# Layer 1's projections in a new order, opened by token halves over two units of weights

## What is computed

```python
u  = _modulate(_rms_norm(h, norm_mix[l]), shm, scm)      # 256 tokens
uc = _modulate(_rms_norm(hc, norm_mix[l]), cshm, cscm)   # 256 context tokens
p = u @ w_in[l]                                          # queries, keys and values
q_w, q_g, q_n = _split_q(p[..., :1024])
k_w, v_w, k_g, v_g, k_n, v_n = _split_kv(p[..., 1024:])
kv_c = uc @ w_in[l][:, 1024:]                            # last layer: no queries of the context
q_g, k_g = _rms_norm(q_g, q_norm_glob[l]), _rms_norm(k_g, k_norm_glob[l])
ck_g = _rms_norm(ck_g, k_norm_glob[l])
q_w, k_w = _rope(q_w, cos, sin), _rope(k_w, cos, sin)
q_g, k_g = _rope(q_g, cos, sin), _rope(k_g, cos, sin)
...                                                      # window, global and neighbourhood attention
h = h + gm * (jnp.concatenate([y_w, y_g, y_n], axis=-1) @ w_out[l])
```

## Time and profile before

| what | value |
|---|---|
| median of 3 runs | 2045.58 us (2043.97 to 2045.92) |
| profiled execution, first to last instruction | 2042.0 us |
| around the span (median less span) | 3.6 us |
| PE busy | 1990.4 us, 97% of the span |
| DVE, ACT, POOL busy | 1410.1, 817.7, 221.7 us |
| mean granted TensorE clock | 0.993 of full speed |
| DMA | 314.41 MB, mean 154 GB/s |

### The profile page before, as it was taken

One profiled execution on the slowest core, in us unless ns is written; L12 is line 12 of the kernel. 1 busy time (PEld: TensorE's weight loads), 2 busy tenths in 40 slices (PEclk: granted clock), 3 DMA queues, 4 the chain that ended last, 5 costly groups with the idle time before them and its releaser, 6 DMA issues.

```text
span 2042.0 us, 28261 instructions
## 1 busy us (share of the span) xinstructions
PE 1990.4 (97%) x11270; PEld 1699.9 (83%) x11270; DVE 1410.1 (69%) x1985; ACT 817.7 (40%) x1182; POOL 221.7 (11%) x129
## 2 busy tenths in 40 slices
PE   8989999999999999999999999999999999999998
PEld 7977778888888887589888888988888888689998
DVE  6879997878867668845888867566664346865444
ACT  6353676222222336944222222322222234764443
POOL 0010001000001002520000001000000101333431
PEclk9999999999999999999999999999999999999999
DMA  6558994666545362024566555366654335125654
GB/s 200 160 171 267 300 347 116 188 178 186 162 137 166 116 166 70 2 63 114 156 185 177 152 160 151 84 175 195 187 164 131 91 114 162 42 83 145 186 164 146
DMA packets 415048, 314.41 MB, mean 154 GB/s; under 512 B 27559, under 2 KB 373686, under 8 KB 414918
## 3 DMA queue, kind: packets, MB, share of 16 engines
q1 hardware_dynamic: 375344, 236.97, 39.9%
q10 hardware_dynamic: 39574, 75.64, 12.0%
HBM read 311.52 MB, written 1.05 MB: 153 GB/s over the span
## 4 chain that ended last, share of the span: by engine, by line
PE 85%; DVE 8%; ACT 4%; issue 2%; DMA 1%; SPq 0%; DVEq 0%; ACTq 0%
PE ps L2311 25%; PE ps L2313 24%; PE ps L2312 24%; DVE w_lo L1340 3%; PE ps L2304 2%; PE ps L3156 2%; PE ps L3123 2%; ACT w_hi L779 1%; DVE ada_acc L1366 1%; DVE tmp_a L1425 1%; PE ps L2888 1%; DVE u_lo L1433 1%; PE ps L2890 1%; PE ps L2889 1%; PE ps L2919 1%
## 5 line engine op out<-in xcount | busy, mean ns | idle before, releaser
L2311 PE MATMUL ps<-u_hi,w_hi 128*128 128x512 f32 (+2 forms) x2112 | 736.5, 349 | 15.7 <-DVE u_lo L1433 7.7
L2312 PE MATMUL ps<-u_lo,w_hi 128*128 128x512 f32 (+2 forms) x2112 | 727.2, 344 | 0.0
L2313 PE MATMUL ps<-u_hi,w_lo 128*128 128x512 f32 (+2 forms) x2112 | 727.2, 344 | 0.0
L1340 DVE TENSOR_TENSOR w_lo<-raw,w_hi 128x2048 fp32r<-128x2048 f32 (+1 forms) x214 | 449.5, 2101 | 219.2 <-ACT w_hi L779 219.0
L779 ACT CAST w_hi<-raw 128x2048 fp32r<-128x2048 f32 (+1 forms) x213 | 371.0, 1743 | 413.3 <-PE ps L2313 379.0
L2311 PEld LDWEIGHTS ps<-u_hi,w_hi 128*128 128x128 f32 x2112 | 401.2, 190 | 70.3 <-DVE w_lo L1340 9.9
L2313 PEld LDWEIGHTS ps<-u_hi,w_lo 128*128 128x128 f32 x2112 | 401.2, 190 | 47.2
L2312 PEld LDWEIGHTS ps<-u_lo,w_hi 128*128 128x128 f32 x2112 | 401.4, 190 | 45.4
L1366 DVE SCALAR_TENSOR_TENSOR ada_acc<-ada_w,sc_c,ada_acc 128x512 f32<-128x512 f32 x448 | 318.0, 765 | 6.4 <-DVE ada_acc L1363 1.0
L899 ACT ACTIVATE tmp_a<-ps 128x512 f32<-128x512 f32 (+1 forms) x88 | 47.9, 544 | 559.6 <-PE ps L2313 417.7
L2311 PE MATMUL ps<-hf_hi,w_hi 128*128 128x512 f32 (+1 forms) x770 | 268.5, 349 | 0.1
(11 more groups left out here) (423 smaller groups left out, 2065.7 us busy)
## 6 DMA issues: line engine op xcount, KB each, us to landing
ada_w<-in_w_ada ACTq DMA_DIRECT2D x144, 512.0 KB, 3.8
raw<-in_w_ffn_gate SPq DMA_DIRECT2D x88, 512.0 KB, 4.0
raw<-in_w_ffn_up SPq DMA_DIRECT2D x88, 512.0 KB, 5.3
raw<-in_w_in SPq DMA_DIRECT2D x52, 512.0 KB, 5.0
raw<-in_w_ffn_down SPq DMA_DIRECT2D x64, 384.0 KB, 3.6
raw<-in_w_ffn_down SPq DMA_DIRECT2D x64, 320.0 KB, 4.2
raw<-in_w_expert_down SPq DMA_DIRECT2D x26, 512.0 KB, 6.3
raw<-in_w_expert_gate SPq DMA_DIRECT2D x25, 512.0 KB, 5.4
```

What stands on the lines that cost most here:

```text
L1340: tt(low, full, high.bitcast(F32), ALU.subtract).then_inc(lo_done.sem, 1)
L2311: mm(acc, w1, m_hi, start=(first and i == 0), stop=False)
L2312: mm(acc, w1, m_lo, start=False, stop=False)
L2313: ins = mm(acc, w2, m_hi, start=False, stop=(last and i == n - 1))
```

## The change

An explicit order of units replaces the natural one in layer 1: two key/value units (4 and 5), the four query units, the three other key/value units. Layer 0 keeps its order. In layer 1 the first two units are now 512 wide and are opened by `open_two`, as in layer 0; `second=False`, `CTX_ROWS` and both `context_rows` go. The groups `q` and `kv` keep their sizes, so `kv` now holds two query units and three key/value units, and the places of `att`, `sink` and the bias table in SP's queue stay behind the fourth and behind the seventh unit.

```diff
-        def taken_with(tile):
-            return 0 if tile < KA else (tile - KA) // 2 + 1
+        QKV_ORDER = [[0, 1, 2, 3, 4, 5, 6, 7, 8], [4, 5, 0, 1, 2, 3, 6, 7, 8]]
+        def taken_with(l, tile):
+            return max(QKV_ORDER[l].index(tile // 2) - 3, 0)
...
-        CTX_ROWS = ((0, 3), (3, 7), (7, 8), (8, 8))
...
-                linear(L["q"], a["w_in_2"][l], 0)
+                linear(L["q"], a["w_in_2"][l], 0, None, QKV_ORDER[l][0:4])
...
-                linear(L["kv"], a["w_in_2"][l], D, range(0, 3))
+                linear(L["kv"], a["w_in_2"][l], 0, range(0, 3), QKV_ORDER[l][4:])
...
-                linear(L["kv"], a["w_in_2"][l], D, range(3, 5))
+                linear(L["kv"], a["w_in_2"][l], 0, range(3, 5), QKV_ORDER[l][4:])
...
-                halves_norm(f"l{l}b", l, 3, end_of(L["f1b"]), next_two(L["f1b"]), second=not last)
-
-                def context_rows(i):
-                    k0, k1 = CTX_ROWS[i]
-                    high_rows("l1b", 72 + 24, 1, k0, k1)
-                linear(L["q"], ada=None if last else "q", behind=context_rows if last else None)
+                halves_norm(f"l{l}b", l, 3, end_of(L["f1b"]), next_two(L["f1b"]))
+                linear(L["q"], ada=None if last else "q")
...
+                def take(n, acc):
+                    i = QKV_ORDER[l][n]
+                    return to_queries(i, acc) if i < 4 else to_keys(i - 4, acc)
+
+                linear(L["q"], take, None if last else "q")
...
-                linear(L["kv"], to_keys, tail=None if last else 15, behind=pre_work, keep_last=2, units=4)
+                linear(L["kv"], lambda i, acc: take(4 + i, acc), tail=None if last else 15, behind=pre_work, keep_last=2, units=4)
...
-                linear(L["q"], TQ, ada=None if last else "q", opening=f"l{l}b")
+                widths = [TQ if i < 4 else T2 for i in QKV_ORDER[l]]
+                linear(L["q"], T2, ada=None if last else "q", opening=f"l{l}b", widths=widths)
...
-                linear(L["kv"], T2, tail=None if last else 15, behind=pre_work, units=4)
+                linear(L["kv"], T2, tail=None if last else 15, behind=pre_work, units=4, widths=widths[4:])
```

More of the change, by code:

```diff
@@ L1196, in pre_square @@
                     Tn = T2 if t == KB else TQ
-                    act.wait_ge(acc_free.sem, acc_free.at(L["kv"]["g0"] + taken_with(t)))
+                    act.wait_ge(acc_free.sem, acc_free.at(L["kv"]["g0"] + taken_with(l, t)))
                     if i >= 2:
@@ L2080, in _ @@
                 ffn_down(L["f1b"], add_gated(T2), "l1_f1b" if last else "f1b", keep=2)
-                halves_norm(f"l{l}b", l, 3, "mix", L["f1b"], add_half_down(L["f1b"], f"l{l}b"), next_two(L["f1b"]),
-                            second=not last)
+                halves_norm(f"l{l}b", l, 3, "mix", L["f1b"], add_half_down(L["f1b"], f"l{l}b"), next_two(L["f1b"]))
                 gates(l, 3, 1.0)
-                def context_rows(i):
-                    k0, k1 = CTX_ROWS[i]
-                    rows_from("l1b", 72 + 24, 1, k0, k1)
                 def to_queries(i, acc):
@@ L2097, in to_queries, with to_keys @@
                     return ins
-                linear(L["q"], to_queries,
-                       None if last else "q", behind=context_rows if last else None)
+                def to_keys(i, acc):
+                    return nc.vector.tensor_copy(proj2[:, 8 + 2 * i:10 + 2 * i, :], acc)
+                def take(n, acc):
+                    i = QKV_ORDER[l][n]
+                    return to_queries(i, acc) if i < 4 else to_keys(i - 4, acc)
+                linear(L["q"], take, None if last else "q")
                 def pre_work(i):
@@ L2128, in pre_work @@
                             dve.wait_ge(A["roped"].sem, A["roped"].at(pre_count(("rope",), n + 1)))
-                def to_keys(i, acc):
-                    return nc.vector.tensor_copy(proj2[:, 8 + 2 * i:10 + 2 * i, :], acc)
-                linear(L["kv"], to_keys, tail=None if last else 15, behind=pre_work, keep_last=2, units=4)
+                linear(L["kv"], lambda i, acc: take(4 + i, acc), tail=None if last else 15, behind=pre_work, keep_last=2, units=4)
                 N = len(A["units"])
@@ L2463, in close_down, with linear @@
                     ins.then_inc(unit_done.sem if q else first_closed.sem, 1)
-            def linear(stg, T, ready=None, squares=None, ada=None, tail=None, behind=None, i0=0, c0=0, opening=None, units=None):
+            def linear(stg, T, ready=None, squares=None, ada=None, tail=None, behind=None, i0=0, c0=0, opening=None, units=None,
+                       widths=None):
                 for i in range(i0, stg["units"] if units is None else units):
+                    T = widths[i] if widths else T
                     u, g = stg["u0"] + i, stg["g0"] + i
@@ L3076, in pre_work @@
                             pe.wait_ge(A["pre_act"].sem, A["pre_act"].at(n - 2))
-                        pe.wait_ge(acc_free.sem, acc_free.at(L["kv"]["g0"] + taken_with(t)))
+                        pe.wait_ge(acc_free.sem, acc_free.at(L["kv"]["g0"] + taken_with(l, t)))
                         if what == "norm":
```

## The result

The changed kernel takes 2054.07 us, the median of five runs (2052.58 to 2056.11), against 2045.47 (2043.89 to 2045.92) for the kernel before on the same chip: a ratio of 1.0048, interval 1.0038 to 1.0059. It is 0.5% slower. The profiled executions differ by 2051.2 - 2042.0 = 9.2 us of span.

| | before | after | difference |
|---|---|---|---|
| start of the projections | 1669.29 | 1668.68 | -0.61 |
| stage | 93.95 | 103.19 | +9.24 |
| from there to the end | | | +0.57 |
| span | 2042.0 | 2051.2 | +9.2 |

A forecast was written before the change was run, and what follows sets the result against it. PE, busy 97% of 2042.0 us, was taken as the bound. Later start of KB's mean 6.8, low clock 1.7, less 0.3 given back, made +8.2; with 3.6 us around the span, 2053.8 us, range 2049.0 to 2057.5.

The forecast's parts named there:

- Opening and query units: Start of layer 1's projections: opening of 26.24 us as in layer 0, then four query units at 5.79 us each.
- the insert: Ahead of the seventh unit: mean matmuls of tiles 3 and 4 and first value transposes, priced at 1.2 us.
- The value with two ends: Weight transfers feeding the four query units: costed at nothing, up to 1 us if one lands like the slowest.
- The shift of SP's row: SP's queue: seventh unit's transfers, bias table and eighth unit's transfers all come 7.15 us later.
- The wait: PE ahead of KB's mean matmul: idles 10.3 us for KB's square and starts that matmul 6.8 us later than before.
- The hold of the low part: DVE's low part of the eighth unit, beside POOL's add: still takes 4.22 us; escaping would save 1.9 us.
- The clock: PE behind the long wait, in the eighth unit: a window at half speed costing 1.7 us.
- Given back: Behind the eighth unit: PE's earlier waits on ACT and DVE, as the 0.44 us one, shrink by 0.3 us.
- (a): Rival, eighth unit: no hold, KB's square done by 1730.85, PE keeps its 3.45 us gain; 2042.1 us; 6%.
- (b): Rival, eighth unit: smaller hold, clock stays up and low part misses POOL's add; 2050.2 us with both; 10%.
- (c): Rival: low clock longer than in any row, or query units' transfers late by 1 us each; 2057 to 2063 us; 6%.
- (d): Rival: query units not emptied or normed in time, a tile's norm waits; hidden, under 0.5 us; no separate chance.

The follow-up runs named there:

- a_bias_late: Changed kernel with layer 1's 24 bias table transfers issued behind the ninth unit's weights instead of between the seventh's and eighth's: 2045.72 us, ratio 1.0011.
- a_bias_18: Changed kernel with 18 of layer 1's 24 bias table transfers left in place and 6 issued behind the ninth unit's weights: 2049.72 us, ratio 1.0031.
- a_kb_later: Changed kernel with KB's norm and the second value transposes moved in layer 1 from ahead of the eighth unit to behind it: 2052.03 us, ratio 1.0040.
- b_bias_late: Kernel before the change, with layer 1's bias table transfers moved behind the ninth unit's weights: 2045.0 us, ratio 1.0004.
- a_fill: Changed kernel with 11 matmuls, results unused, added on PE ahead of KB's mean matmul to keep it busy in the wait: 2052.11 us, ratio 1.0035.
- a_late_pieces: Changed kernel with the bias table behind the ninth unit and POOL's mask addition cut into six pieces in the attention: 2041.78 us, ratio 0.9988.
- a_early_pieces: Changed kernel with all bias table issues ahead of the fifth unit's weights and POOL's mask addition cut into six pieces: 2047.48 us, ratio 1.0009.

## Why the prediction was right

The forecast was +8.2 us on the profiled span and 2053.8 us; measured were +9.2 on the span and 2054.07 us. That the time agrees within 0.3 us where the span is 1.0 off is luck. The prediction added 3.6 us around the span as a constant of the kernel; in after the median of the runs stands 2.9 us over the span. In every run with both numbers the span is only 1.7 to 1.9 us shorter than the time, so the rest of the 3.6 is most likely that one execution was profiled and another is the median. The mechanism holds all the same. Point by point:

- **Opening and query units.** 26.24 us forecast, about 26.26 found (to 1694.94); 5.79 us forecast for a unit, 5.76 found; 1.2 for the insert, 1.22 found. No query unit waited for a transfer. The value with two ends, up to 1 us for a slow landing, was nothing.
- **The shift of SP's row.** The seventh unit's issue was forecast for 1705.8 and came at 1705.25, with a start 0.61 us earlier. The table took 16.54 us (16.23 before).
- **The wait.** 10.3 us forecast, 10.22 found; KB's mean matmul, counted from the start of the projections, 6.88 us later against 6.8 forecast. That the queue makes this wait is shown by a_bias_late (gone) and a_bias_18 (shorter as expected), and a_kb_later splits it into 7.2 us of transfers and 3.1 us of KB's own chain.
- **The hold of the low part.** Taken as it was (4.22), found 4.08, again ending 2.15 us behind POOL's addition (1737.51 and 1735.36). In a_bias_18 the low part was over (1733.57) before the addition began (1736.86) and took 2.29 us. But nothing was saved there, since a later product was caught for longer. A low part that started first while the addition came in beneath it stands in b_bias_late: it kept its 2.29 us, and the addition took longer. So there the trace bears out what the Trainium skill has in SBUF — State Buffer, section "SBUF: two separate sides" (the first to start keeps the ports for its whole instruction).
- **The clock.** Forecast 1.7 us, found 9.24 - 6.88 = 2.36, and 2.28 by a_fill. This term was mis-sized. The window was priced from the earlier trace rows, the shorter of the two there; here the low clock lasts 5.0 us past the wait. 1.34 us of it fall on the insert (1740.57 to 1743.12 is 2.55 us; 1.21 before), about 1.0 on the start of the eighth unit. The Trainium skill's warning (TensorE: Matmul & The Clock Gate, section "HAM oscillation — how this bites in real kernels") held, and a_fill, which keeps PE busy through the wait, shows its price in this kernel. The prediction set a wait of 1.61 us (full speed) against one of 2.06 (low clock) and put 10.3 us far beyond both. For 10 us that was right, but the length of the last wait doesn't decide the shorter cases: a_bias_18 kept full speed after 2.27 us.
- **Given back.** 0.3 us were forecast from the 0.44 us wait at the earlier trace rows. It is 0.44 in after too: nothing came back. With the clock's 0.66 this makes the 1.0 us that the span is above the forecast.
- **Rivals.** (a) asked for KB's square 10 us earlier than computed. Only the moved table gave this, in an edit that the change didn't contain, and then 2041.78 us came out of it with the pieces and 2045.72 without: the 2042.1 of (a) is what this order is worth once two further obstacles are taken away. (b) needed the clock to stay up and the low part to escape; neither happened. (c) asked for late query units or a low clock longer than in any row. The 5.0 us are longer than the 4.40 of the earlier trace rows, so its second condition came true, but it cost 0.7 us more than forecast, and the price of (c) began at 3.2 us more in all. (d), a tile's norm that waits, was hidden as computed: no wait of PE in the stage names one except KB's square.

Open: whether the 0.57 us behind the stage and the 0.61 ahead of it mean anything. The thirteen profiled executions have the same work ahead of the projections, and their starts lie between 1668.09 and 1670.47, so 0.6 us is within what one execution differs from another. Not tried: leaving the table's transfers out, or KB's later place together with a moved table.

## What to carry to other kernels

When an order is changed to feed the opening faster, follow every queue that is shared with it, to the transfers that are issued between the moved ones: what was covered by three wide pieces of work may now be covered by one, and the later piece pays. Price an idle time of TensorE with its length and the half-rate stretch behind it, and look first at the smallest part of a reorder by itself; here an early split gave 2.8 of 3.5 us. A long operation of GpSimd, moved to get a queue out of the way, should be cut into pieces before it meets VectorE's two-input work.

## What the runs showed of the hardware

- A long addition on GpSimd (6.8 us) stretched ordinary 32-bit VectorE operations on two tensors that started behind it: 0.42 to 7.00 us in a_bias_late, 0.48 to 6.45 in a_bias_18, 2.29 to 4.08 in after. A low part that started ahead of it kept its 2.29 us, and a reciprocal of one tensor beneath it kept its 3.35 (b_bias_late). In six pieces of 1.27 us the addition cost PE nothing.
- 24 small transfers of the bias table in one run took 15.8 to 16.5 us to issue, 0.66 to 0.69 us each (a_late_pieces, after), and the transfers of 512 KB issued right behind them landed late: after 6.2 to 9.5 us in the thirteen profiles, where the seventh unit's took at most 5.3.
- After 10.22 us of idle time the granted clock was 0.52 for 5.0 us; it had fallen to 0.50 while PE still waited (0.59 from 1735 to 1736 us, 0.50 until the wait ended).
- For short waits the length of the last one didn't decide. Low clock followed 2.06 us, 3.38 in a_early_pieces and 3.80 in a_bias_late; full speed followed 1.61 us and 2.27 in a_bias_18. The same work isn't always granted the same clock either: behind a wait of 0.81 us that stands in both, PE ran at 0.50 from 934 to 936 us in after and at 1.00 in before. So a low clock behind a short wait should be looked for in more than one profile.
